# A two-block transformer kernel on one core: each engine's order of work taken from a drawn sketch instead of one common list

## The chip, the cores and the metric

The kernel runs on one core of a Trainium2 chip. Five engines work side by side, each through its own fixed instruction stream: TensorE (PE, matrix products), VectorE (DVE), ScalarE (ACT), GpSimd (POOL) and SyncE (SP, which issues the DMA transfers). They meet only at semaphores. The metric is the device time of one launch in microseconds.

## The reference

The input `x` is 1024 wide with 512 tokens, a context adds 256 tokens. `first_block` is one layer:

```python
x = x + 0.5 * rms_norm(swiglu(rms_norm(x, ffn1_pre_g), ffn1_w_gu, ffn1_w_down), ffn1_post_g)
y = hybrid_mixer(rms_norm(x, mix_pre_g), ...)    # RG-LRU recurrence beside windowed attention
x = x + rms_norm(y, mix_post_g)
x = x + 0.5 * rms_norm(swiglu(rms_norm(x, ffn2_pre_g), ...), ffn2_post_g)
```

The second block has two layers on latents and context. Each is a mixer and a feed-forward network with a `layer_norm` (mean, variance, root) behind each sum, shifts, scales and gates from a conditioning vector (`modulate`), and a mixer that is retention in the first layer and neighbourhood attention in the second. All products are fp32.

## The kernel before

**Tiling.** Activations lie transposed: 128 partitions hold one of 8 chunks of the width (`c`), the free axis holds tokens. A product of 1024 inputs to 128 outputs is an `mm` item: 8 steps `k`, each of three matmuls (`products`, L1463 to L1465), since every fp32 operand is held as a high and a low part and the products low·high, high·low, high·high are added in one PSUM bank. Tokens come as one group of 512 or two of 256 (`s`).

**Who does what.** SP loads weights into a ring of three raw tiles. ACT casts a raw tile to its high part (`prep`, L1723); DVE (L2018) or POOL (L2477) subtracts to get the low part (`prep_lo`). TensorE multiplies. DVE or ACT drain the PSUM bank: `up` and `gate` make the hidden tile (L2149 product, L2152 its low part, L1787 the activation), `down_f` (L2162) and `gated` (L2173) take the outputs. DVE also works out the modulation, 192 operations `ada` (L2107, 128x1024), spread through the program.

**Norms.** A norm over the width is a chain across three engines. Squares (ACT L1731, L1733) are added up (DVE `sum`, L2038). On TensorE `root_sum` (L1549) adds over the partitions by short matmuls, ACT takes the root (L1738), DVE turns and spreads it (`root_diag`, L2044, L2048), and TensorE's `root_row` (L1557) puts it in a bank. From there DVE scales (`norm_apply` L2079, `norm_add` L2086, or `ln_apply` L2092), and the sends (ACT L1744, L1768, L1770; DVE L2066, L2098) write the next matmul's operand `t_h`, high and low. A layer norm has a `mean` (TensorE L1538, L1540) ahead.

**What sets the order.** `schedule()` emits one Python list `items`. The norm chains are generators that yield hand-written delays in microseconds; `tick(us)` is called as the matmul work is emitted and steps each chain whose delay is over, `force` steps a chain to its end where its result is needed. `root`, which places `root_sum`, `root_diag` and `root_row`, reads:

```python
    put("root_sum", inst=inst, s=s, eps=eps, bank=b, before=before, col=i % 4 * 2)
    yield 2.4
    ...
    put("root_diag", inst=inst, s=s, off=off, after=after, col=i % 4 * 2)
    ...
    yield 1.2
    put("root_row", inst=inst, s=s, off=off, bank=b)
```

All five programs then walk that one list with `for it in items: if it.kind in part: part[it.kind](it)`. So an item's place in the list is its place on every engine that has a part in it; an engine never passes an item whose semaphore isn't there yet. The stretches of the program, in order: f1 (to about 386 us), the hybrid mixer, f2, retention, f3, neighbourhood attention, f4.

Of the kernel before, what the change touches and what calls it, by code (L numbers as in the profile page):

```python
# [63 lines left out]
ONCE = (0, 2048, 8704)  # L64
VSTART = {0: 0, 128: 1, 256: 2, 384: 3, 64: 4, 192: 5, 320: 6}
# [33 lines left out]
class Lane:  # L99


    def __init__(self, engine, board):
        self.engine, self.board, self.passed = engine, board, {}

    def wait_ge(self, name, key):
        if not self.board.real:
            return
        s = self.board[name]
        v = s.when[key]
        if self.passed.get(name, 0) < v:  # L110
            self.passed[name] = v
            self.engine.wait_ge(s.sem, v)

# [18 lines left out]
def schedule():  # L132
# [4 lines left out]
    lows, adds = [], []  # L137
    where, low, closing, closed, coming = {}, {}, set(), {}, itertools.count()
# [227 lines left out]
    def sum_add(inst, s, c, tile, ready, square, after=(), late=False):  # L366
        it = dict(inst=inst, s=s, c=c, tile=tile, ready=ready, square=square, after=list(after), off=0, keys=[])
        if square:
# [129 lines left out]
    def ffn(f, gu, dn, parts, segs, subs, ends, ver, down, scaled, between=None, first=6, whole=1, steps=together, begun=None, per=32, ahead=None):  # L498
# [13 lines left out]
        for pi, size in enumerate(parts):  # L512
# [13 lines left out]
            def up_post(k, pi=pi, over_hid=over_hid):  # L526
                def post(g):
# [3 lines left out]
                        turned=f == "f3" and pi == len(parts) - 1 and g.n == 512,  # L531
                        los=[(f, pi, k, s) for s in range(g.t0 // 256, (g.t0 + g.n) // 256)])
# [64 lines left out]
    def first_mixer():  # L597
# [27 lines left out]
        def scores(n):  # L625
# [3 lines left out]
            put("att_scores", n=n, before=before, after=[w_free[2 * n], w_free[2 * n + 1]])  # L629
# [201 lines left out]
    def retention():  # L831
# [18 lines left out]
        def queries_keys(h):  # L850
            first = {}

            def post(g, w, k):
# [4 lines left out]
                else:  # L858
# [6 lines left out]
                    put("qk_rope", w=w, h=h, g0=first["g"], b0=first["bank"], g=g.id, bank=g.bank, offs=offs, slots=before, after=ov["qk"])  # L865

# [35 lines left out]
        def finish(h, t0, n):  # L902
# [4 lines left out]
            put("ret_finish", h=h, t0=t0, n=n, bank=b, before=seat(b, "drain_act", ("ret_rs", h, t0)), offs=[v[0] for v in t[t0]], after=rs_after)  # L907

# [469 lines left out]
def sync_program(e, w, S, m, dram, items, loads):  # L1378
# [22 lines left out]
    for it in items:  # L1401
# [59 lines left out]
def tensor_program(e, w, S, m, items):  # L1461
# [239 lines left out]
    for it in items:  # L1701
# [4 lines left out]
def scalar_program(e, w, S, m, items):  # L1706
# [289 lines left out]
    for it in items:  # L1996
# [4 lines left out]
def vector_program(e, w, S, m, items):  # L2001
# [136 lines left out]
    def up(it):  # L2138
# [8 lines left out]
        if it.turned:  # L2147
            out, s, ps = t.rearrange("p (c r) -> p c r", r=8), s.rearrange("p (r c) -> p c r", c=64), ps.rearrange("p (r c) -> p c r", c=64)
        e.tensor_tensor(out, s, ps, ALU.mult).then_inc(  # L2149
            *S["drain_dve"].of(it.g, ("up", it.f, *it.los[0][1:3], it.t0)))  # L2150
        w.wait_ge("hid_hi", it.los[0])
# [120 lines left out]
    def att_scores(it):  # L2272
        nk = P if it.n == 0 else 2 * P
        w.wait_ge("d_misc", "mask1")
        for kv in range(2):
# [67 lines left out]
    def qk_rope(it):  # L2343
# [3 lines left out]
        for half in range(2):  # L2347
# [9 lines left out]
            e.tensor_tensor(u, u, v, ALU.subtract if half == 0 else ALU.add).then_inc(*S["qk"].of((h, wq, half)))  # L2357
        wait_all(it.after)
# [36 lines left out]
    def ret_finish(it):  # L2395
        h, t0, n, rs = it.h, it.t0, it.n, m.rs(it.t0, it.n)
# [3 lines left out]
        e.tensor_tensor(a, a, m.tmp(it.offs[2], n), ALU.add).then_inc(*S["ret_dve"].of(("s", h, t0)))  # L2400
        w.wait_ge("drain_act", ("ret_rs", h, t0))
# [17 lines left out]
    def na_scores(it):  # L2419
        for hd in range(2):  # L2420
            k, key = it.at[hd], (it.half, it.p, hd)
            w.wait_ge("na_ps", ("s", *key))
            w.wait_ge("bm", (it.half, it.c, BKIND[it.b], hd))
# [21 lines left out]
    def na_o(it):  # L2445
# [7 lines left out]
            "mod_send": mod_send, "norm_apply": norm_apply, "norm_add": norm_add, "ln_apply": ln_apply, "ln_send": ln_send, "ada": ada, "ada_add": ada_add, "gate": gate, "up": up,  # L2453
            "down_f": down_f, "gated": gated, "mix_lambda": mix_lambda, "mix_pad": mix_pad, "scaled": scaled, "conv": conv, "rec_l": rec_l, "rec_c": rec_c,
            "rec_e": rec_e, "rec_g": rec_g, "att_scores": att_scores, "att_probs": att_probs, "att_out": att_out, "mix_apply": mix_apply, "mix_lo": mix_lo,
            "ret_setup": ret_setup, "ret_decay": ret_decay, "qk_rope": qk_rope, "qk_ctx": qk_ctx, "rows_split": rows_split,
            "ret_score": ret_score, "ret_low": ret_low, "ret_y": ret_y, "ret_split": ret_split, "ret_copy": ret_copy,
            "ret_finish": ret_finish, "na_scores": na_scores, "na_probs": na_probs, "na_y": na_y, "na_o": na_o}
    w.wait_ge("d_par", 0)
    for it in items:  # L2460
# [4 lines left out]
def gpsimd_program(e, w, S, m, items):  # L2465
# [40 lines left out]
    for it in items:  # L2506
# [19 lines left out]
def build_program(nc, ins, out):  # L2526
    with ExitStack() as ctx:
# [10 lines left out]
        def run(program, e, *a):  # L2538
            program(e, Lane(e, S), S, m, *a)

        programs = ((sync_program, (dram, items, loads)), (tensor_program, (items,)), (scalar_program, (items,)),
                    (vector_program, (items,)), (gpsimd_program, (items,)))
        for program, a in programs:
            run(program, Quiet(), *a)
# [4 lines left out]
        def _(e):  # L2549
            run(programs[0][0], e, *programs[0][1])  # L2550

        @block.tensor
        def _(e):
            run(programs[1][0], e, *programs[1][1])

        @block.scalar
        def _(e):
            run(programs[2][0], e, *programs[2][1])

        @block.vector  # L2560
        def _(e):
            run(programs[3][0], e, *programs[3][1])

        @block.gpsimd
        def _(e):
            run(programs[4][0], e, *programs[4][1])
# [95 lines left out]
```

## Time and profile before

| | |
|---|---|
| runs | 2977.07, 2978.41, 2978.04 us |
| median | 2978.04 us |
| span of the profiled execution | 2969.8 us |
| median less that span | 8.2 us |
| mean granted TensorE clock | 0.986 of full |
| DMA | 268.84 MB, mean 91 GB/s |

No time beside its span is recorded for the profiled execution itself; the 8.2 us between the span (first to last instruction) and the median of the runs is taken as what lies around it.

A row of a timeline reads: start, length, engine, line and operation, output <- inputs with partitions x elements, and in brackets the idle time of the engine just before with what ended it. A matmul's length is that of its own pipeline; two that follow each other start closer together than they are long.

### The profile page before, as it was taken

The numbers are of one execution on the slowest core, as the hardware profiler recorded it, in microseconds if no ns is written. First come the engines' busy times: TensorE is split into PE (matmuls) and PEld (weight loads), VectorE is DVE, ScalarE is ACT, GpSimd is POOL, SyncE is SP. The second block draws the span as 40 slices with busy tenths as digits, with TensorE's granted clock in tenths as the row PEclk, the third lists the DMA queues.
The fourth block names the chain that finished last, engine by engine and source line by source line (L and its number), as shares of the span: only waits on it lengthen the run. The fifth ranks groups of instructions, "written<-read, shape, count | busy, mean of one in ns | idle before, by whom it ended". The sixth has DMA issues, their size and how long they took to land.

```text
span 2969.8 us, 40717 instructions
## 1 busy us (share of the span) xinstructions
PE 2860.4 (96%) x16352; PEld 2484.7 (84%) x16352; DVE 1536.3 (52%) x2689; ACT 1079.2 (36%) x1873; POOL 540.6 (18%) x287
## 2 busy tenths in 40 slices
PE   8999989999999999999999899999999989999998
PEld 7888886988878888888888888888887777988887
DVE  5667468656674643434446543543564525642224
ACT  5322247543323542423324622112245435442222
POOL 2333200023332011110111011111102212122210
PEclk9999999999999999999999999999999999999999
DMA  4554312225443111121111032322422121133331
GB/s 163 170 163 156 113 59 79 79 83 177 148 160 114 66 56 58 37 71 36 57 57 50 30 106 94 116 92 84 142 70 77 47 71 49 65 93 101 99 99 36
DMA packets 84715, 268.84 MB, mean 91 GB/s; under 512 B 9008, under 2 KB 16560, under 8 KB 84144
## 3 DMA queue, kind: packets, MB, share of 16 engines
q1 hardware_dynamic: 84528, 266.25, 27.8%
q8 instruction: 129, 2.11, 0.3%
q14 instruction: 58, 0.48, 0.1%
HBM read 262.54 MB, written 2.10 MB: 89 GB/s over the span
## 4 chain that ended last, share of the span: by engine, by line
PE 61%; DVE 4%; ACT 2%; issue 1%; DMA 0%; DVEq 0%; ACTq 0%
PE ps L1463 19%; PE ps L1464 19%; PE ps L1465 19%; PE ps L1691 1%; PE ps L1675 1%; PE ps L1664 1%; DVE t_m L2038 1%; ACT t_whi L1723 1%; DVE t_m L2061 0%; ACT t_h L1770 0%; DVE t_wlo L2018 0%; PE ps L1557 0%; ACT t_tmp L1970 0%; DVE t_x L2061 0%; DVE t_x L2173 0%
## 5 line engine op out<-in xcount | busy, mean ns | idle before, releaser
L1463 PE MATMUL ps<-t_h,t_whi 128*128 128x512 f32 (+1 forms) x2320 | 810.5, 349 | 12.8 <-DVE t_h L2066 9.5
L1464 PE MATMUL ps<-t_h,t_wlo 128*128 128x512 f32 (+1 forms) x2320 | 805.6, 347 | 0.0
L1465 PE MATMUL ps<-t_h,t_whi 128*128 128x512 f32 (+1 forms) x2320 | 804.6, 347 | 0.0
L2477 POOL TENSOR_TENSOR t_wlo<-t_raw,t_whi 128x1024 fp32r<-128x1024 f32 (+3 forms) x144 | 350.9, 2437 | 1465.4 <-ACT t_whi L1723 1465.2
L1463 PEld LDWEIGHTS ps<-t_h,t_whi 128*128 128x128 f32 x2320 | 442.6, 191 | 74.6 <-issue 16.1
L1464 PEld LDWEIGHTS ps<-t_h,t_wlo 128*128 128x128 f32 x2320 | 442.7, 191 | 54.3 <-issue 1.0
L1465 PEld LDWEIGHTS ps<-t_h,t_whi 128*128 128x128 f32 x2320 | 442.3, 191 | 54.1
L1723 ACT CAST t_whi<-t_raw 128x1024 fp32r<-128x1024 f32 (+3 forms) x322 | 321.0, 998 | 306.9 <-PE ps L1465 258.7
L1463 PE MATMUL ps<-t_hid,t_whi 128*128 128x256 f32 (+1 forms) x1298 | 423.0, 326 | 6.6 <-DVE t_hid L2152 4.3
L1464 PE MATMUL ps<-t_hid,t_wlo 128*128 128x256 f32 (+1 forms) x1298 | 420.3, 324 | 0.0
L1465 PE MATMUL ps<-t_hid,t_whi 128*128 128x256 f32 (+1 forms) x1298 | 419.5, 323 | 0.0
L2018 DVE TENSOR_TENSOR t_wlo<-t_raw,t_whi 128x1024 fp32r<-128x1024 f32 (+3 forms) x178 | 219.3, 1233 | 261.0 <-ACT t_whi L1723 260.6
L2107 DVE CUSTOM_DVE_ANT_0 t_m<-t_raw,t_m 128x1024 f32<-128x1024 f32 x192 | 302.3, 1611 | 49.9 <-DMA t_raw<-in_ada 39.3
L1463 PEld LDWEIGHTS ps<-t_hid,t_whi 128*128 128x128 f32 x1298 | 248.5, 191 | 28.4 <-DVE t_hid L2152 4.5
L1464 PEld LDWEIGHTS ps<-t_hid,t_wlo 128*128 128x128 f32 x1298 | 248.6, 192 | 19.1
L1465 PEld LDWEIGHTS ps<-t_hid,t_whi 128*128 128x128 f32 x1298 | 248.3, 191 | 19.1
L2149 DVE TENSOR_TENSOR t_tmp<-t_m,ps 128x512 f32<-128x512 f32 (+1 forms) x121 | 72.7, 601 | 310.3 <-PE ps L1465 265.4
L1796 ACT CAST t_hid<-t_tmp 128x512 fp32r<-128x512 f32 (+1 forms) x121 | 65.7, 543 | 368.0 <-DVE t_tmp L2149 368.0
L2152 DVE TENSOR_TENSOR t_hid<-t_tmp,t_hid 128x512 fp32r<-128x512 f32 (+1 forms) x121 | 92.4, 764 | 73.9 <-ACT t_hid L1796 73.9
L2483 POOL TENSOR_TENSOR t_m<-t_m,t_tmp 128x512 f32<-128x512 f32 (+1 forms) x49 | 62.7, 1280 | 328.4 <-ACT t_m L1787 328.4
L1463 PE MATMUL ps<-t_wlo,t_h 128*128 128x512 f32 x264 | 103.9, 394 | 0.4 <-DVE t_m L2425 0.4
L1463 PE MATMUL ps<-t_h 128*128 128x512 f32 (+1 forms) x256 | 94.0, 367 | 10.5 <-DVE t_m L2162 10.5
(290 smaller groups left out, 4142.2 us busy)
## 6 DMA issues: line engine op xcount, KB each, us to landing
t_raw<-in_gu SPq DMA_DIRECT2D x176, 512.0 KB, 3.3
t_raw<-in_ada SPq DMA_DIRECT2D x96, 512.0 KB, 3.4
t_raw<-in_dn SPq DMA_DIRECT2D x52, 512.0 KB, 3.7
t_raw<-in_dn SPq DMA_DIRECT2D x24, 384.0 KB, 3.3
t_raw<-in_ret_v SPq DMA_DIRECT2D x16, 512.0 KB, 4.3
t_raw<-in_ret_qk SPq DMA_DIRECT2D x16, 512.0 KB, 3.4
t_raw<-in_ret_g SPq DMA_DIRECT2D x16, 512.0 KB, 3.3
t_raw<-in_ret_o SPq DMA_DIRECT2D x16, 512.0 KB, 3.8
```

The lines of the kernel that those rows point to most:

```text
L1463: e.matmul(out, whi, xlo, start=first, stop=False, skip_group_check=shared)
L1464: e.matmul(out, wlo, xhi, start=False, stop=False, skip_group_check=shared)
L1465: return e.matmul(out, whi, xhi, start=False, stop=last, skip_group_check=shared)
L1664: done = e.matmul(m.PS[:, hd, o:o + 256], m.na_q(it.c, it.b * P, P)[pp], m.na_k(it.c, keys, 256)[pp], start=True, stop=True, skip_group_ch ...
L1723: e.copy(m.block(0, it.slot, math.prod(it.shape)), m.raw(it)).then_inc(*S["hi"].of(j))
L1796: e.copy(m.hid(0, it.k, it.pitch, it.t0, it.n), m.tmp(it.off, it.n)).then_inc(*S["hid_hi"].of(it.los[0]))
L2018: e.tensor_tensor(m.block(1, it.slot, n), m.raw(it), m.block(0, it.slot, n), ALU.subtract).then_inc(*S["lo_dve"].of(j))
L2107: e.tensor_tensor_reduce(m.at(ADA_OUT + who * 1024, 1024), m.RAW[:, it.raw % NR, :], m.cond(who), 1.0, 0.0, ALU.mult, ALU.add, m.mod(it.la ...
L2149: e.tensor_tensor(out, s, ps, ALU.mult).then_inc(*S["drain_dve"].of(it.g, ("up", it.f, *it.los[0][1:3], it.t0)))
L2152: e.tensor_tensor(m.hid(1, it.k, it.pitch, it.t0, it.n), t, m.hid(0, it.k, it.pitch, it.t0, it.n), ALU.subtract).then_inc(*S["hid_lo"].of( ...
L2477: e.tensor_tensor(m.block(1, it.slot, n), m.raw(it), m.block(0, it.slot, n), ALU.subtract).then_inc(*S["lo_pool"].of(j))
L2483: e.tensor_tensor(s, s, m.rs(it.t0, it.n), ALU.mult).then_inc(*S["gate_pool"].of(it.key, *((it.f, "rs", h) for h in halves(it.t0, it.n))))
```

## The change

A new class `Plan` first draws the five programs without emitting anything: every engine call is recorded as an `Op` with the events it waits for and a length from a formula in its shape. Then `arrange` works back from TensorE's order to give each operation a time at which it is due, and `run` plays the five engines forward. Each time an engine is free it takes, among the items that could begin, the one due soonest. Operations of one `(kind, inst, s)` keep their order among themselves; SP's and TensorE's main order stay. `mean`, `root_sum` and `root_row` float on TensorE: they are taken as soon as what they wait for is there, also between two steps `k` of an `mm` item (`between`). The real programs then follow these orders. Some items are split so that their halves can be placed apart (`up` and `up_lo`, `qk_rope` and `qk_lo`, `ret_finish` and `ret_recip`), some waits that the common order had implied are written out (`acc_read`, `ready_x`, `misc_free`, `nsink`, `bm`), and `mm` waits for its low weights behind the wait for its operand.

```diff
+    FLOATING = ("mean", "root_sum", "root_row")
...
+        n = math.prod(out.shape[1:])
+        if self.engine == "tensor":
+            if name == "transpose" or n == 1:
+                takes = 109
+            elif a[1].dtype == F32R:
+                takes = max(n / 2.4 + 13.3, 109)
+            else:
+                takes = 2 * max(2 * n / 2.4 + 2.5, 109)
...
+            lasts = takes + 165
+        elif self.engine == "scalar":
+            takes = 110 + 0.8 * n
+            lasts = takes + 95
...
+        elif self.engine == "vector":
+            takes = 6.55 * n if name == "reciprocal" and n > 64 else 1150 if n == 1024 else 65 + 1.05 * n
+            if name == "scalar_tensor_tensor":
+                takes += 60
+            lasts = takes + 85
+        elif self.engine == "gpsimd":
+            takes = 150 + 2.2 * n
+            lasts = takes + 60
+        else:
+            takes, lasts = 480, 3300
...
+                        some = [q for q in heads[engine] if q and q[0][0].at <= t and self.opens(q[0])]
+                        if engine in ("scalar", "vector", "gpsimd"):
+                            some = [q for q in some if q[0][0].due < t + 60000]
...
+                        if engine == "tensor":
+                            q = min(some, key=lambda q: self.family(q[0][0]) == ("main",))
+                        else:
+                            q = min(some, key=lambda q: q[0][0].due)
...
+                    if op.table is not None and op.table != table:
+                        table, takes, lasts = op.table, takes + 1283, lasts + 1283
...
     def mm(it):
         out = m.PS[:, it.bank, 0:it.n]
-        w.wait_ge(it.lo, it.w)
         for k in range(it.nk):
+            if k:
+                for x in w.between(it, k):
+                    part[x.kind](x)
             xhi, xlo = moving(it, k)
             if k == 0:
+                w.wait_ge(it.lo, it.w)
                 wait_all(it.before)
...
-    for it in items:
+    for it in w.turns(items):
         if it.kind in part:
             part[it.kind](it)
```

The numbers of instructions stay as they were on PE, DVE, POOL and SP; ACT has 56 `ACT_TABLE_LOAD` where it had 49. Lines of the changed kernel are 270 to 285 higher: the products are L1733 to L1735, `root_row` L1830, `prep_lo` L2291, `sum` L2311, `down_f` L2438.

**VectorE at the end of f1.** The rows are DVE's, `L2162` (now `L2438`) being the drains of the last output columns, whose banks the mixer's first products wait for, and `L2018` (now `L2291`) low parts of the mixer's weights. Before:

```order
L2066 SCALAR_TENSOR_TENSOR t_h<-t_x,t_par,t_h 128x256 [waits h_hi]
L2086 TENSOR_TENSOR t_x<-t_x,t_m 128x256 [waits f_scaled]
L2066 SCALAR_TENSOR_TENSOR t_h<-t_x,t_par,t_h 128x256 [waits h_hi]
L2162 TENSOR_TENSOR t_m<-t_m,ps 128x256 [waits ps]
L2038 TENSOR_TENSOR t_m<-t_m,t_tmp 128x256 [waits sq,acc]
L2018 TENSOR_TENSOR t_wlo<-t_raw,t_whi 128x1024 [waits hi,d_ring2]
L2066 SCALAR_TENSOR_TENSOR t_h<-t_x,t_par,t_h 128x256 [waits h_hi] x2
L2162 TENSOR_TENSOR t_m<-t_m,ps 128x256 [waits ps]
L2038 TENSOR_TENSOR t_m<-t_m,t_tmp 128x256 [waits sq,acc]
L2018 TENSOR_TENSOR t_wlo<-t_raw,t_whi 128x1024 [waits hi,d_ring0]
L2162 TENSOR_TENSOR t_m<-t_m,ps 128x256 [waits ps]
L2038 TENSOR_TENSOR t_m<-t_m,t_tmp 128x256 [waits sq,acc] x2
```

and with the change:

```order
L2339 SCALAR_TENSOR_TENSOR t_h<-t_x,t_par,t_h 128x256 [waits h_hi]
L2352 SCALAR_TENSOR_TENSOR t_m<-t_m,t_par,ps 128x256 [waits drain_dve]
L2438 TENSOR_TENSOR t_m<-t_m,ps 128x256 [waits ps]
L2339 SCALAR_TENSOR_TENSOR t_h<-t_x,t_par,t_h 128x256 [waits h_hi]
L2359 TENSOR_TENSOR t_x<-t_x,t_m 128x256 [waits f_scaled]
L2291 TENSOR_TENSOR t_wlo<-t_raw,t_whi 128x1024 [waits hi,d_ring2]
L2339 SCALAR_TENSOR_TENSOR t_h<-t_x,t_par,t_h 128x256 [waits h_hi]
L2438 TENSOR_TENSOR t_m<-t_m,ps 128x256 [waits ps]
L2291 TENSOR_TENSOR t_wlo<-t_raw,t_whi 128x1024 [waits hi,d_ring0]
L2311 TENSOR_TENSOR t_m<-t_m,t_tmp 128x256 [waits sq]
L2311 TENSOR_TENSOR t_m<-t_m,t_tmp 128x256 [waits sq,acc_act]
L2311 TENSOR_TENSOR t_m<-t_m,t_tmp 128x256 [waits sq,acc] x4
```

Before, each of the last two drains stands behind its own low part of weights, and a sum behind every drain; now one low part is left between the drains of the excerpt, and the sums come together behind the last drain.

**TensorE at the start of f3.** `root_row` of the first layer norm's variance (`l00v`, first 256 tokens) stood between the last product of retention's output (`t_hid`) and the first of f3 (`t_h`). Before:

```order
L1463 MATMUL ps<-t_hid,t_whi 128x256
L1464 MATMUL ps<-t_hid,t_wlo 128x256
L1465 MATMUL ps<-t_hid,t_whi 128x256
L1557 MATMUL ps<-t_tmp,t_con 128x128 [waits root_dve]
L1557 MATMUL ps<-t_tmp,t_con 128x128
L1463 MATMUL ps<-t_h,t_mw 128x256 [waits drain_dve,lo_pool,h_lo]
L1464 MATMUL ps<-t_h,t_mw 128x256
```

and with the change, where the main products are the same and the first of f3 follows the last of retention at once:

```order
L1733 MATMUL ps<-t_h,t_whi 128x256
L1734 MATMUL ps<-t_h,t_wlo 128x256
L1735 MATMUL ps<-t_h,t_whi 128x256
L1830 MATMUL ps<-t_tmp,t_con 128x128 [waits root_dve]
L1830 MATMUL ps<-t_tmp,t_con 128x128
L1733 MATMUL ps<-t_h,t_mw 128x256 [waits h_lo]
L1734 MATMUL ps<-t_h,t_mw 128x256
```

It stands 48 matmuls of 256 columns later in the main order.

**VectorE in the neighbourhood attention.** `L2425` (now `L2709`) adds the bias to a block's scores, `L2435` (now `L2719`) scales the probabilities, `L2018` (now `L2291`) is the low part of weights. Before:

```order
L2425 ISA t_m 128x1
L2425 ISA t_m<-ps,t_m 128x512 [waits bm,na_ps]
L2425 ISA t_m 128x1
L2425 ISA t_tmp,t_m<-ps,t_m 128x512 [waits h_lo,hid_lo,bm,na_ps]
L2425 ISA t_m 128x1
L2425 ISA t_tmp,t_m<-ps,t_m 128x512 [waits bm,na_ps]
L2425 ISA t_m 128x1
L2433 RECIPROCAL t_m<-t_m 128x1 [waits na_act]
L2435 TENSOR_SCALAR t_m<-t_m 128x512 [waits na_dve]
L2433 RECIPROCAL t_m<-t_m 128x1 [waits na_act]
L2435 TENSOR_SCALAR t_m<-t_m 128x512 [waits na_dve]
L2018 TENSOR_TENSOR t_wlo<-t_raw,t_whi 128x1024 [waits hi,d_ring1]
```

and with the change:

```order
L2709 ISA t_m<-ps,t_m 128x512 [waits bm,na_ps]
L2709 ISA t_m 128x1
L2709 ISA t_m<-ps,t_m 128x512 [waits bm,na_ps]
L2709 ISA t_m 128x1
L2717 RECIPROCAL t_m<-t_m 128x1 [waits na_act]
L2719 TENSOR_SCALAR t_m<-t_m 128x512 [waits na_dve]
L2717 RECIPROCAL t_m<-t_m 128x1 [waits na_act]
L2719 TENSOR_SCALAR t_m<-t_m 128x512 [waits na_dve]
L2709 ISA t_tmp,t_m<-ps,t_m 128x512 [waits h_lo,hid_lo,bm,na_ps]
L2709 ISA t_m 128x1
L2709 ISA t_tmp,t_m<-ps,t_m 128x512 [waits bm,na_ps]
L2709 ISA t_m 128x1
```

The first block's probabilities now come ahead of the second block's scores, and the low part that stood behind them follows nine rows later.

## Rows read from the trace of the kernel before

**Rows 1.** Page, part 1: busy time, share of the span and instructions of each engine.

```profile
PE 2860.4 (96%) x16352; PEld 2484.7 (84%) x16352; DVE 1536.3 (52%) x2689; ACT 1079.2 (36%) x1873; POOL 540.6 (18%) x287
```

**Rows 2.** Waits of PE: waiting line <- releaser: us in total, times, longest.

```profile
PE ps L1557 <- DVE t_tmp L2048: 25.0, 11, 7.8
PE ps L1549 <- DVE t_m L2038: 14.5, 6, 4.8
PE ps L1664 <- DVE t_m L2425: 11.5, 6, 4.3
PE ps L1463 <- DVE t_m L2162: 10.5, 1, 10.5
PE ps L1463 <- DVE t_h L2066: 10.0, 2, 9.5
PE ps L1664 <- ACT t_m L1807: 4.8, 1, 4.8
PE ps L1463 <- DVE t_hid L2152: 4.3, 1, 4.3
PE ps L1598 <- ACT t_m L1867: 4.0, 3, 3.2
PE ps L1463 <- DVE t_h L2098: 2.7, 1, 2.7
```

**Rows 3.** Thirteen windows, two and the sum: PE, PEld, DVE, ACT, POOL busy, clock, DMA.

```profile
1644.10:1654.30 10.20, 4.81 (x22) 4.81 (x23) 9.28 (x20) 7.69 (x17) 0.00 (x0) 0.50 0.32 105
...
2958.20:2969.80 11.60, 3.09 (x12) 2.71 (x12) 4.22 (x13) 3.56 (x9) 0.00 (x0) 0.50 0.27 90
sum 82.60, PE 55.45 PEld 51.15 DVE 54.17 ACT 44.49 POOL 6.21; mean PE 4.27 PEld 3.93 DVE 4.17 ACT 3.42 POOL 0.48
```

**Rows 4.** Timeline of PE, 383 to 398 us: start, length, instruction.

```profile
385.77 0.28 PE L1464 MATMUL ps<-t_hid,t_h 128*128 128x256 f32 x1
385.89 0.28 PE L1465 MATMUL ps<-t_hid,t_h 128*128 128x256 f32 x1
...
397.04 0.42 PE L1464 MATMUL ps<-t_h 128*128 128x256 f32 x1
397.25 0.41 PE L1465 MATMUL ps<-t_h 128*128 128x256 f32 x1
```

**Rows 5.** Timeline of DVE and ACT, 390 to 397 us.

```profile
394.98 1.23 DVE L2018 TENSOR_TENSOR t_wlo<-t_raw,t_whi 128x1024 fp32r<-128x1024 f32 x1 [1.15 <-ACT t_whi L1723]
396.12 0.41 DVE L2162 TENSOR_TENSOR t_m<-t_m,ps 128x256 f32<-128x256 f32 x1
...
393.53 0.42 ACT L1733 ACTIVATE t_tmp<-t_m 128x256 f32<-128x256 f32 x1 [1.68 <-DVE t_m L2162]
393.85 1.03 ACT L1723 CAST t_whi<-t_raw 128x1024 fp32r<-128x1024 f32 x1
```

**Rows 6.** Timeline of ACT and DVE, 1644 to 1650 us.

```profile
1644.88 0.24 ACT L1738 ACTIVATE t_st<-ps,t_con 128x2 f32<-128x2 f32 x1
...
1648.76 0.16 DVE L2044 RECIPROCAL t_st<-t_st 128x2 f32<-128x2 f32 x1
```

**Rows 7.** Timeline of PE, end of the program.

```profile
2958.61 1.87 PE L1549 MATMUL ps<-t_con,t_m 128*128 128x1 f32 x8 [4.84 <-DVE t_m L2038]
```

**Rows 8.** Timeline of ACT, 24 to 26 us.

```profile
24.01 1.28 ACT L1787 ACT_TABLE_LOAD   x1
```

**Rows 9.** Groups by form: busy, mean ns of one, idle before and releaser.

```profile
L2107 DVE CUSTOM_DVE_ANT_0 t_m<-t_raw,t_m 128x1024 f32<-128x1024 f32 x192 | 302.3, 1611 | 49.9 <-DMA t_raw<-in_ada 39.3 <-ACT t_m L1714 10.3
L1970 ACT ACTIVATE t_tmp<-t_tmp,t_m 128x512 f32<-128x512 f32 x40 | 28.6, 715 | 22.0 <-DVE t_m L2425 22.0
L2038 DVE TENSOR_TENSOR t_m<-t_m,t_tmp 128x256 f32<-128x256 f32 x132 | 50.3, 432 | 10.5 <-ACT t_tmp L1733 10.5
```

**Rows 10.** Timeline of POOL and DVE, 1610 to 1613 us.

```profile
1610.29 2.40 POOL L2477 TENSOR_TENSOR t_mw<-t_raw,t_mw 128x1024 fp32r<-128x1024 f32 x1 [2.29 <-ACT t_mw L1723]
...
1610.40 2.57 DVE L2038 TENSOR_TENSOR t_m<-t_x 128x256 f32<-128x256 f32 x1
```

More of the change, by code:

```diff
@@ L4 @@
 import numpy as np
+from collections import deque
 from contextlib import ExitStack
@@ L99, with __init__, turns, between @@
 class Lane:
-    def __init__(self, engine, board):
+    def __init__(self, engine, board, order):
         self.engine, self.board, self.passed = engine, board, {}
+        self.order, self.inside = [], {}
+        inner = []
+        for it, piece in order:
+            if piece:
+                self.inside[it.id, piece] = inner
+                for x in inner:
+                    self.order.remove(x)
+                inner = []
+            elif it.kind in Plan.FLOATING:
+                self.order.append(it)
+                inner.append(it)
+            else:
+                self.order.append(it)
+                inner = []
+    def turns(self, items):
+        return self.order
+    def between(self, it, k):
+        return self.inside[it.id, k]
     def wait_ge(self, name, key):
@@ L112, in wait_ge, with insort, __init__, of @@
             self.engine.wait_ge(s.sem, v)
+def insort(some, x):
+    lo, hi = 0, len(some)
+    while lo < hi:
+        mid = (lo + hi) // 2
+        if some[mid] < x:
+            lo = mid + 1
+        else:
+            hi = mid
+    some.insert(lo, x)
+class Mark:
+    def __init__(self, name, plan):
+        self.name, self.plan = name, plan
+    def of(self, *keys):
+        for k in keys:
+            self.plan.made[self.name, k] = self.plan.ops[self.plan.engine][-1]
+        return self, 0
@@ new lines, with __init__, __getattr__, take @@
+class Op:
+    def __init__(self, engine, item, piece, waits, takes, lasts, table):
+        self.engine, self.item, self.piece, self.waits = engine, item, piece, waits
+        self.takes, self.lasts, self.table = takes, lasts, table
+        self.then, self.due, self.at, self.done = [], LATE, 0.0, False
+class Sketch:
+    def __init__(self, plan):
+        self.plan = plan
+    def __getattr__(self, name):
+        def take(*a, **k):
+            if name != "then_inc":
+                self.plan.note(name, k["out"] if "out" in k else a[0], a)
+            return self
+        return take
@@ L367, in sum_add @@
         it = dict(inst=inst, s=s, c=c, tile=tile, ready=ready, square=square, after=list(after), off=0, keys=[])
+        if c < 2 if square else 2 <= c < 4:
+            it["after"] += acc_read.get(s, [])
         if square:
@@ L1700, in tensor_program @@
     w.wait_ge("d_par", 0)
-    for it in items:
+    for it in w.turns(items):
         if it.kind in part:
@@ L1995, in scalar_program @@
     w.wait_ge("d_par", 0)
-    for it in items:
+    for it in w.turns(items):
         if it.kind in part:
@@ L2505, in gpsimd_program @@
     w.wait_ge("d_par", 0)
-    for it in items:
+    for it in w.turns(items):
         if it.kind in part:
@@ L2536, in build_program, with run @@
         items, loads = schedule()
[L2538 to L2544, printed above, removed]
+        programs = (("sync", sync_program, (m, dram, items, loads)), ("tensor", tensor_program, (m, items)),
+                    ("scalar", scalar_program, (m, items)), ("vector", vector_program, (m, items)),
+                    ("gpsimd", gpsimd_program, (m, items)))
+        plan = Plan()
+        plan.draw(programs)
+        order = plan.arrange()
+        def run(k, e):
+            name, program, a = programs[k]
+            program(e, Lane(e, S, order[name]), S, *a)
+        for k in range(5):
+            run(k, Quiet())
         S.again()
```

179 lines of the change are left out of this document (167 added, 12 removed).

## The prediction

> **What bounds the kernel now.** I read the page's busy times first: TensorE is busy 96% of the span, VectorE 52%, ScalarE 36% [rows 1]. So the order of work on the other engines can win only what TensorE loses to waits and to its clock; the 2860.4 us of its own busy time stay, but for the part run slowly.
>
> Second, the waits of TensorE [rows 2]. Nine rows give 87.3 us; thirteen smaller ones, 2.5 the largest, make it 102.3. I sort them by what the change can reach.
>
> - **Floats**: `root_row` 25.0, `root_sum` 14.5, `mean` 0.9 (a small row): 40.4 us. These matmuls stand at a place in TensorE's queue that a delay in microseconds chose, and all main products wait behind them. Some 6.6 lie in the tail, where nothing is left to put ahead (4.84 in one piece [rows 7]). 33.8 are left.
> - **Order stalls** of main products, 52.4: the neighbourhood attention 18.7 (11.5 and 4.8 [rows 2] and 2.4 in small rows), the end of f1 10.5, the mixer some 8 (4.0 on L1598 [rows 2], 3.9 in small rows), retention 5.5 in small rows, the end of f2 4.3, f4's start 2.7, POOL's low parts 2.5.
> - **The start**, 9.5 of the 10.0 on L2066, waits for the first input. It stays.
>
> Third, the clock. Thirteen windows have a granted clock of 0.50, the lower of the two levels (1.2 of 2.4 GHz); the other stretches are at full. In them TensorE is busy 55.45 us, 3.09 of it in the tail [rows 3]. All but one of the windows begin in a wait of TensorE or right behind one. Products of 256 columns start 0.12 us apart at the end of f1 and 0.21 apart behind the 10.5 us wait [rows 4]. So 52.4 us of work outside the tail cost about twice what they should: 26 us are lost to the clock beside the waits.
>
> Fourth, two places show why the waits are there. At the end of f1 the order is a ladder: ScalarE's square waits for VectorE's drain, the next weights' cast stands behind the square, VectorE's low part waits 1.15 us for that cast, and the next drain stands behind the low part, until the last at 396.12 frees TensorE [rows 5]. These rows are the last rung; each is some 3 to 4 us, and none needs the one before. At the start of f3 ScalarE has the root at 1645.12 (1644.88 plus 0.24), yet VectorE takes the reciprocal at 1648.76 [rows 6], since other items stand ahead of it; `root_row` waits 7.8 us, and f3's products behind it.
>
> **The change, part by part.**
>
> *Floats.* `root_row` of f3's first variance goes behind 48 matmuls of 256 columns, 48 x 0.12 = 5.8 us of work at full clock [rows 4] (11.5 us at the 0.24 of half), and VectorE's side is reordered too, so the 7.8 go. Other floats move by up to 72 matmuls either way, most to where their operand is expected. Bounds: nothing if the products that overtake need the float's own result, all 33.8 if it always has cover. I take 28; the 4.80 near the program's start has little to put ahead. Effect: -28.
>
> *Order stalls.* The end of f1: the sums no longer stand among the drains and one low part leaves them, -10.5. In the mixer half, -4; f2's end has its last hidden tile as the true end of a chain, -2; POOL's low parts -2.5; retention and f4's start 0 (chains of the algorithm); the neighbourhood attention a third, -6, since the first block's probabilities now precede the second block's scores, which helps the next products but puts a wait for ScalarE at VectorE's head. Together -25; bounds 0 and -52.
>
> *Waits that come.* ScalarE's first weight cast now stands behind four sends and a square, which may start TensorE about 1 us later. Seven more table loads at 1.28 [rows 8] are 9.0 us on an engine that is 64% idle; between 0 and 9.0 on the path. Float matmuls placed too early are new waits. I take +1 for the start and +5 for the rest.
>
> The Trainium skill, "ScalarE: Activation LUTs", section "What ACT_TABLE_LOAD costs", says that a switch costs a drain besides the load, 2.66 us in all; seven would be 18.6. By that the upper end of this term, and the sum at worst, would be 9.6 us higher.
>
> *Everything else moved* (weights' casts and low parts, ada, drains in the FFNs) costs nothing where TensorE works through columns without waits: f2, f3 and f4 have hardly a row in the waits, since casts and low parts run columns ahead of it. If that cover went, each low part of 1.2 us would show.
>
> *Clock.* 53 of the 86 us of waits outside start and tail go; the clock's 26 go in proportion, 16. Bounds 0 and 26.
>
> Sum: -28 - 25 + 1 + 5 - 16 = -63. The profiled span of 2969.8 becomes 2906.8; with the 8.2 us between span and median, 2978.0 - 63 = **2915 us**.
>
> Best case: 34 of floats, 40 of stalls, 24 of the clock and nothing new, 98 less: 2880.
>
> **Rivals.**
>
> *A: the sketch's lengths are too short.* An item taken as ready is not, and on a real engine all behind it waits. An exp over 128x512 with its accumulated sum is 110+0.8x512 = 520 ns in the sketch; the trace has 715 for the exp alone [rows 9]. VectorE now stands at the reciprocal behind two such exps before it may touch the next block's scores. A VectorE sum that runs beside a POOL low part took 2.57 us [rows 10] against a mean of 0.43 [rows 9]; the sketch has no such term. With 32 block pairs at 2 x 0.2 us, the attention loses 12 us instead of winning 6. Floats then give 20, f1's end 10.5, other stalls 0, the clock 6: -20 - 10.5 + 12 - 6 = -24.5, 2954. For it: these rows. Against: in the FFNs slack of whole columns absorbs it.
>
> The Trainium skill, "GPSIMD Engine Reference", section 8, says that GpSimd shares its SBUF interfaces with VectorE and that VectorE instructions with two SBUF inputs contend with it. By that rule moves onto other neighbours change lengths everywhere, as here; the trace agrees at 1610 us.
>
> *B: VectorE's backlog is the limit where the long floats are.* In the window from 1644.1 it is busy 9.28 of 10.2 us [rows 3]. If the operand `t_h` of f3's products is simply late, the wait moves from `root_row` to them. The two places of that kind have 7.8 and 7.0 us and smaller ones of 2.2; those 17 and 5 of the clock stay: -63 + 22 = -41, 2937.
>
> *C: slower, by `ada`.* Its 192 operations take 1611 ns [rows 9] and 1150 in the sketch. Where one stands right ahead of a drain that TensorE waits for, it makes that 0.46 us late. 192 x 0.46 = 88 us if every one does: 2978 - 63 + 88 = 3003. The place is block 2's FFNs and mixers; it decides from 137 of the 192 (63 / 0.46), and below some 30 it is not seen. Against: TensorE has six banks in turn, so one late drain is not waited for, and before no wait is put down to an `ada`.
>
> *D: the change does not do what it says.* The orders come out so alike that only places off the path move: 2978. Against: the order of all five stalls above is seen to differ.
>
> **How the numbers follow.** Forecast 0.60, A 0.16, B 0.12, C 0.07, D 0.05. A measurement of this kernel tells about 0.2%, 6 us, from no change. Faster by more: forecast, B and A, 0.88; same: D, 0.05; slower: C, 0.07. The range takes the best case as its lower end, 2880. Above it must leave out no more than 0.2: C, D and half of A are that, so it ends a little above A's time, at 2960. The forecast's own range is 2880 to 2945.
>
> **What would show it.** Right: TensorE's waits fall from 102.3 to about 55; the row of `root_row` on its releaser falls from 25 to under 5; the 10.5 us wait at the end of f1 is gone; the windows of half clock fall to five or so; busy time of VectorE and ScalarE as before, plus 9 us of table loads. A shows as TensorE waits on the scores (L2709) of the attention growing, with VectorE idle on ScalarE's exp; B as waits of L1733 for `t_h` near 1650 and 2220 us; C as many small waits on drains with `ada` just before them. Wrong altogether, if TensorE's waits stay above 90 us or new rows over 5 us appear in the FFNs.

## The result and the profile after

The changed kernel takes **2897.89 us** (median of 4 runs, 2897.53 to 2898.70) against 2978.09 us for the kernel before (4 runs), a ratio of 0.9736 with a 95% interval of 0.9724 to 0.9748. It is 80 us faster; 63 were forecast, with a range that holds the time.

The page of the changed kernel, part 1, to be read beside [rows 1]:

```profile
PE 2842.3 (98%) x16352; PEld 2469.1 (85%) x16352; DVE 1549.7 (53%) x2689; ACT 1093.3 (38%) x1880; POOL 542.6 (19%) x287
```

TensorE's busy time is 18.1 us less with the same instructions, which is the clock. VectorE's is 13.4 us more and ScalarE's 14.1, 9.0 of that the seven table loads. TensorE's waits (line <- releaser: us in total, times, longest), to be read beside [rows 2]:

```profile
PE ps L1733 <- DVE t_wlo L2291: 11.6, 1, 11.6
PE ps L1733 <- DVE t_hid L2428: 9.3, 4, 8.0
PE ps L1822 <- DVE t_m L2311: 6.2, 4, 4.8
PE ps L1830 <- DVE t_tmp L2321: 4.8, 5, 1.2
PE ps L1937 <- DVE t_m L2709: 2.5, 6, 0.7
...
PE ps L1813 <- DVE t_m L2311: 1.9, 3, 1.0
PE ps L1811 <- DVE t_m L2311: 1.8, 1, 1.8
...
PE ps L1937 <- ACT t_m L2080: 0.8, 1, 0.8
...
PE ps L1733 <- DVE t_m L2438: 0.7, 1, 0.7
```

TensorE's idle time is 47.6 us in all, from 102.3; the rows of this view hold 46.8 of it, the rest are gaps too short for a row. The floats (L1822, L1830, L1813, L1811) have 14.7 left of 40.4, and the largest piece of that is the tail's 4.8, as before [rows 7]. The 10.5 at the end of f1 is 0.7 (L2438). The attention's scores (L1937) fell from 11.5 and 4.8 to 2.5 and 0.8. Two rows are larger: the start, 11.6 from 9.5, and a new one of 8.0 in f1, for `up_lo` (L2428), the low part of a hidden tile.

The windows at the half clock (busy of PE, PEld, DVE, ACT, POOL, then the granted clock), to be read beside [rows 3]:

```profile
340.20:350.30 10.10, 3.88 (x10) 2.78 (x11) 7.57 (x12) 2.32 (x4) 2.11 (x1) 0.50 0.44 156
517.60:524.40 6.80, 6.80 (x33) 6.80 (x33) 3.08 (x10) 2.12 (x5) 0.00 (x0) 0.50 0.00 0
1579.00:1582.50 3.50, 3.50 (x19) 3.50 (x18) 3.13 (x9) 2.08 (x6) 0.00 (x0) 0.52 0.00 0
2883.00:2896.90 13.90, 3.09 (x12) 2.71 (x12) 6.56 (x20) 4.78 (x13) 0.00 (x0) 0.50 0.23 75
sum 34.30, PE 17.27 PEld 15.79 DVE 20.34 ACT 11.30 POOL 2.11; mean PE 4.32 PEld 3.95 DVE 5.08 ACT 2.82 POOL 0.53
```

Four windows are left of thirteen. Outside the tail, 14.2 us of products run at 1.2 GHz in place of 52.4, so some 7 us are lost and not 26. One of them comes with the new wait and one (1579.0) behind a wait of 1.8 us; one (517.6) comes in a stretch where TensorE is busy throughout and had waited only 0.7 us in one piece, some 2 us before, and why it is there stays open.

**Where the new wait comes from.** VectorE (start, length, instruction, idle before and releaser):

```profile
336.73 0.17 DVE L2467 TENSOR_SCALAR t_m<-t_m 128x4 f32<-128x4 f32 x1 [14.05 <-ACT t_m L2092]
...
340.74 0.17 DVE L2488 TENSOR_SCALAR t_m<-t_m 128x4 f32<-128x4 f32 x1
340.82 0.69 DVE L2409 TENSOR_TENSOR t_m<-ps,t_tmp 128x512 f32<-128x512 f32 x1
341.43 0.68 DVE L2422 TENSOR_TENSOR t_tmp<-t_m,ps 128x512 f32<-128x512 f32 x1
342.02 3.42 DVE L2291 TENSOR_TENSOR t_wlo<-t_raw,t_whi 128x1024 fp32r<-128x1024 f32 x2
345.36 0.68 DVE L2428 TENSOR_TENSOR t_hid<-t_tmp,t_hid 128x512 fp32r<-128x512 f32 x1
```

and ScalarE in the same stretch:

```profile
334.13 1.05 ACT L1996 CAST t_whi<-t_raw 128x1024 fp32r<-128x1024 f32 x1 [4.39 <-PE ps L1735]
335.19 1.28 ACT L2092 ACT_TABLE_LOAD   x1
336.49 0.21 ACT L2092 ACTIVATE t_m<-t_m 128x4 f32<-128x4 f32 x1
```

The item `mix_lambda`, the decay of the mixer's recurrence, has one exp on ScalarE and 21 dependent operations of 0.2 us after it on VectorE, all one block that nothing may interrupt. It isn't needed until the mixer. VectorE reached it early and stood 14.05 us at its head for an exp that ScalarE's order has behind two casts, each of which waits 4.39 us for TensorE. Then the block, the last gate and two low parts stood ahead of `up_lo`, and TensorE, out of work at 338.1, went on at 346.1.

### The profile page after: what moved, and what is told of

Its sections match the earlier page's. It is cut to its first block, busy times and chain, and to the rows that moved or that the text cites. A ratio compares the mean times of both kernels' runs of the same rounds, so it can differ in the third digit from the quotient of the medians.

```text
span 2896.9 us, 40773 instructions
## 1 busy us (share of the span) xinstructions
PE 2842.3 (98%) x16352; PEld 2469.1 (85%) x16352; DVE 1549.7 (53%) x2689; ACT 1093.3 (38%) x1880; POOL 542.6 (19%) x287
## 4 chain that ended last, share of the span: by engine, by line
PE 90%; DVE 4%; ACT 4%; issue 1%; DMA 0%; POOL 0%; DVEq 0%; ACTq 0%; SPq 0%; POOLq 0%
PE ps L1733 29%; PE ps L1734 28%; PE ps L1735 28%; PE ps L1937 1%; PE ps L1964 1%; PE ps L1948 1%; ACT t_whi L1996 1%; DVE t_m L2311 1%; DVE t_wlo L2291 1%; PE ps L1822 1%; ACT t_h L2043 0%; PE ps L1830 0%; ACT t_tmp L2041 0%; DVE t_x L2449 0%; DVE t_m L2334 0%
## 5 line engine op out<-in xcount | busy, mean ns | idle before, releaser
L1733 PE MATMUL ps<-t_h,t_whi 128*128 128x512 f32 (+1 forms) x2320 | 807.4, 348 | 12.4 <-DVE t_wlo L2291 11.6
L1735 PE MATMUL ps<-t_h,t_whi 128*128 128x512 f32 (+1 forms) x2320 | 802.5, 346 | 0.0
L2761 POOL TENSOR_TENSOR t_wlo<-t_raw,t_whi 128x1024 fp32r<-128x1024 f32 (+3 forms) x144 | 342.2, 2377 | 1501.6 <-ACT t_whi L1996 1501.6
L1733 PEld LDWEIGHTS ps<-t_h,t_whi 128*128 128x128 f32 x2320 | 440.3, 190 | 71.9 <-issue 18.2
L1735 PEld LDWEIGHTS ps<-t_h,t_whi 128*128 128x128 f32 x2320 | 440.1, 190 | 54.2
L1733 PE MATMUL ps<-t_hid,t_whi 128*128 128x256 f32 (+1 forms) x1298 | 422.1, 325 | 0.6 <-DVE t_hid L2428 0.6
L1735 PE MATMUL ps<-t_hid,t_whi 128*128 128x256 f32 (+1 forms) x1298 | 419.5, 323 | 0.0
L2291 DVE TENSOR_TENSOR t_wlo<-t_raw,t_whi 128x1024 fp32r<-128x1024 f32 (+3 forms) x178 | 216.6, 1217 | 129.3 <-ACT t_whi L1996 129.0
L1733 PEld LDWEIGHTS ps<-t_hid,t_whi 128*128 128x128 f32 x1298 | 248.2, 191 | 21.5 <-issue 0.9
L1735 PEld LDWEIGHTS ps<-t_hid,t_whi 128*128 128x128 f32 x1298 | 248.1, 191 | 19.2
L2428 DVE TENSOR_TENSOR t_hid<-t_tmp,t_hid 128x512 fp32r<-128x512 f32 (+1 forms) x121 | 114.8, 953 | 33.7 <-ACT t_hid L2069 33.3
L1733 PE MATMUL ps<-t_wlo,t_h 128*128 128x512 f32 x264 | 103.6, 393 | 0.0
L1734 PE MATMUL ps<-t_whi,t_h 128*128 128x512 f32 x264 | 102.9, 390 | 0.0
L1735 PE MATMUL ps<-t_whi,t_h 128*128 128x512 f32 x264 | 102.8, 389 | 0.0
```

Of the source, the lines that this page charges most:

```text
L1733: e.matmul(out, whi, xlo, start=first, stop=False, skip_group_check=shared)
L1734: e.matmul(out, wlo, xhi, start=False, stop=False, skip_group_check=shared)
L1735: return e.matmul(out, whi, xhi, start=False, stop=last, skip_group_check=shared)
L2291: e.tensor_tensor(m.block(1, it.slot, n), m.raw(it), m.block(0, it.slot, n), ALU.subtract).then_inc(*S["lo_dve"].of(j))
L2428: e.tensor_tensor(m.hid(1, it.k, it.pitch, it.t0, it.n), t, m.hid(0, it.k, it.pitch, it.t0, it.n), ALU.subtract).then_inc(*S["hid_lo"].of( ...
L2761: e.tensor_tensor(m.block(1, it.slot, n), m.raw(it), m.block(0, it.slot, n), ALU.subtract).then_inc(*S["lo_pool"].of(j))
```

## The experiments

Each run is compared with runs of the kernel before on the same chip in the same session; those medians were 2975.0, 2976.4, 2977.2 and 2976.4 us. The runs of e1, e4 and e8 spread over 5 to 9 us, those of e2, e3, e7 and e10 over 3 to 5.4, those of the others over 1.3 at most.

**e1, all orders from the list.** In `family`, and floats off:

```diff
+        if op.engine in ('scalar', 'vector', 'gpsimd'):
+            return ("main",)
...
-    FLOATING = ("mean", "root_sum", "root_row")
+    FLOATING = ()
```

> The changed kernel with every engine in the order of the one list and no float; the split items, the written-out waits and the later wait for low weights stay. Theory 1 (the new orders make the whole gain): as before, 2978 within 2 us, TensorE's waits some 102 us with the 10.5 and 7.8 us ones back. Rival (a part of the gain comes from the split items or the moved wait for low weights): 2 to 10 us faster than before.

Measured: 2976.1 us, ratio 1.0005 (0.9995 to 1.0014). The waits of 10.5, 7.9 and 6.9 us are back:

```profile
PE ps L1832 <- DVE t_tmp L2323: 23.5, 11, 7.9
...
PE ps L1735 <- DVE t_m L2440: 10.5, 1, 10.5
```

The split items, the written-out waits and the later wait for low weights cost and give nothing that this interval, some 3 us to either side, can show; the gain is order, that of the other engines' queues and that of the floats.

**e2, the floats alone.** The same lines in `family`, `FLOATING` kept.

> ScalarE, VectorE and GpSimd in the list's order; mean, root_sum and root_row float on TensorE. Theory 1 (floats and order add up, 28 us of waits and some 9 of clock by the floats): about 2941. Rival (the floats' operands come late because VectorE's order holds them, so moving the matmul alone only takes the products out from behind it and soon they want the norm themselves): 2955 to 2970, with waits of the products for t_h in place of root_row's.

Measured: 2951.2 us, ratio 0.9930 (0.9913 to 0.9946), between the two expectations. The floats' own waits fell, but the products took some of them over. Waits of TensorE in e2:

```profile
PE ps L1735 <- DVE t_h L2341: 11.8, 2, 9.1
PE ps L1735 <- DVE t_m L2440: 11.6, 1, 11.6
...
PE ps L1824 <- DVE t_m L2313: 7.7, 3, 4.8
PE ps L1735 <- DVE t_hid L2430: 7.6, 2, 4.3
...
PE ps L1735 <- DVE t_wlo L2293: 3.6, 2, 2.9
PE ps L1832 <- DVE t_tmp L2323: 3.0, 3, 1.1
```

`root_row` (L1832) has 3.0 of 25.0 us, `root_sum` (L1824) 7.7 of 14.5; `mean` grew from 0.9 to 3.9, so the floats together went from 40.4 to 14.6. New are 2.7 for `t_h` (11.8 with the start's 9.1), 3.3 for `t_hid` and 2.1 for `t_wlo` beyond what stood in their rows: products that had been held back by a float now reach the next late operand sooner.

**e3, the orders alone.** Only `FLOATING = ()`.

> ScalarE, VectorE and GpSimd in the sketch's order, made with mean, root_sum and root_row at the list's places on TensorE. Theory 1: the order stalls' 31 us and their clock go, floats' waits stay near 30: about 2937. Rival (the sketch's order on VectorE brings root_diag early enough that even fixed floats hardly wait): 2910 to 2920, floats' waits under 15 us.

Measured: 2912.1 us, ratio 0.9795 (0.9781 to 0.9810): the rival's side, though the floats' waits are 17.8 us, a little above its 15. Waits of TensorE in e3:

```profile
PE ps L1822 <- DVE t_m L2311: 13.3, 4, 4.8
PE ps L1733 <- DVE t_wlo L2291: 11.0, 1, 11.0
PE ps L1733 <- DVE t_hid L2428: 11.0, 3, 9.9
...
PE ps L1830 <- DVE t_tmp L2321: 3.8, 3, 1.6
```

`root_row` at its old place waits 3.8 us in place of 25.0, since VectorE takes the reciprocal when the root is there. At the start of f3 it is this row, 0.30 us behind the root, where before it was 3.6 us late [rows 6]:

```profile
1624.23 0.17 DVE L2317 RECIPROCAL t_st<-t_st 128x2 f32<-128x2 f32 x1 [0.30 <-ACT t_st L2011]
```

The new wait of the changed kernel is here too, as 9.9 us (L2428). So the two remedies overlap. Floats alone give 24 us, orders alone 63, both 80: with the other engines in order the floats have only 14 us (2912.1 to 2897.9) left to win.

**e4, ScalarE's order alone.** `family` returns `("main",)` for VectorE and GpSimd, no floats.

> Only ScalarE in the sketch's order; VectorE and GpSimd in the list's, no floats. Theory 1 (VectorE's queue is what delays TensorE, ScalarE is 36% busy): little, 2965 to 2980. Rival (the ladder at the end of f1 is broken on ScalarE, by the cast that no longer stands behind the square): the 10.5 us wait shrinks to under 4, some 2960.

Measured: 2959.4 us, ratio 0.9957 (0.9942 to 0.9973); the rival was right. From TensorE's waits in e4:

```profile
PE ps L1832 <- DVE t_tmp L2323: 27.6, 9, 9.3
...
PE ps L1735 <- DVE t_m L2440: 3.9, 1, 3.9
...
PE ps L1939 <- ACT t_m L2082: 0.8, 1, 0.8
```

Beside e1, the wait at the end of f1 fell from 10.5 to 3.9, and one of 4.7 in the attention, a copy of ScalarE (`rows_copy`) that stood behind other work, to 0.8. An engine that is 36% busy delayed TensorE by the order of its queue. Against that, `root_row`'s waits grew from 23.5 to 27.6 us and the start's from 9.7 to 11.3. The orders of VectorE and GpSimd beside ScalarE's list were not run. What they do is read from e4 and e3, which both have ScalarE in the sketch's order and no floats: with them `root_row`'s waits go from 27.6 to 3.8 us. VectorE's share and GpSimd's are not told apart.

**e5, the exp earlier.** After `arrange`:

```diff
+        acts = order["scalar"]
+        at = [n for n, (it, _) in enumerate(acts) if it.kind == "mix_lambda"][0]
+        x = acts.pop(at)
+        preps = [n for n in range(at) if acts[n][0].kind == "prep"]
+        acts.insert(preps[-2], x)
```

> The changed kernel, only ScalarE's exp of the recurrence's decay (mix_lambda, L2092) two weight casts earlier. Theory (the new 8.0 us wait at 346 us is VectorE standing 14 us at its head for that exp, and then doing 21 small operations and two low parts ahead of the last gate of f1): VectorE waits in its own idle time, the 8.0 us wait and the half clock behind it (3.9 us window, about 2 us lost) go: 2888. Rival (the wait is for the block's two low parts, which any order puts there, or for the weights' transfer): above 2894.

Measured: 2890.7 us (2890.4 to 2891.1), 7.2 less than the changed kernel (e6, whose time is that of the changed kernel, has 2898.4 in the same session). VectorE's head and TensorE's row for `t_hid` in e5:

```profile
325.42 0.17 DVE L2467 TENSOR_SCALAR t_m<-t_m 128x4 f32<-128x4 f32 x1 [3.17 <-ACT t_m L2092]
```

```profile
PE ps L1733 <- DVE t_hid L2428: 3.0, 4, 1.0
```

The 14.05 us at the head are 3.17, and the 8.0 us wait is 1.0 at most. The cause is shown: one exp of 0.21 us at a place in ScalarE's queue too late for the place that VectorE's queue gives the block. Moving VectorE's block to a later place instead was not run.

**e6, the start on ScalarE.** The setup activation and the first cast are moved to the front of ScalarE's order.

> The changed kernel, ScalarE's setup activation with its table load and the first weight cast put first again. Theory (the start's wait grew from 9.5 to 11.6 since the table load now waits for x and a cast stands behind four sends): TensorE starts 2 us earlier, 2896. Rival (the start is bound by x's transfer, which varies): no change, 2898.

Measured: 2898.4 us, no change. ScalarE was 2 us earlier, but TensorE's first wait is still 11.4, for VectorE's low part: VectorE's order has four sends ahead of it.

```profile
8.46 1.67 DVE L2339 SCALAR_TENSOR_TENSOR t_h<-t_x,t_par,t_h 128x256 fp32r<-128x256 f32 x4 [5.24 <-ACT t_h L2017]
10.05 1.22 DVE L2291 TENSOR_TENSOR t_wlo<-t_raw,t_whi 128x1024 fp32r<-128x1024 f32 x1
```

Neither theory: it isn't the transfer, and not ScalarE alone. e10 puts both engines back.

**e7, lengths from the trace.** In `note`:

```diff
+            takes += 85 * sum(hasattr(k.get(x), "dtype") for x in ("scale", "bias"))
+            if "accum_out" in k:
+                takes += 200
...
+            if name == "tensor_tensor_reduce":
+                takes += 360 if n == 1024 else 85
```

> The sketch's lengths as the trace has them: ada 1510 ns start to start in place of 1150, 85 ns for each per-partition scale or bias on ScalarE, 200 for an accumulated sum. Theory 1 (the orders are insensitive to such errors, since work is columns ahead): within 4 us of 2898. Theory A (wrong lengths put items at the head before they are ready): 6 to 15 us faster.

These lengths are nearer, not true everywhere: an exp over 128x512 with its accumulated sum is 805 ns in them, where the trace of the kernel before has it and its read 0.72 us from start to start; and the 1510 ns of `ada` are a mean over undisturbed and disturbed ones.

Measured: 2890.5 us (2888.4 to 2893.7), 7.4 less: theory A. The 8.0 us wait stayed; the floats' waits went. Those of e7 that are left:

```profile
PE ps L1827 <- DVE t_m L2316: 4.8, 1, 4.8
...
PE ps L1816 <- DVE t_m L2316: 1.8, 1, 1.8
PE ps L1835 <- DVE t_tmp L2326: 1.1, 1, 1.1
PE ps L1818 <- DVE t_m L2316: 0.9, 2, 0.7
```

8.6 us, 6.6 of them the tail's, from 14.7.

**e8 and e9, lengths too short.** All lengths of the three engines in the sketch times 0.7; e9 has `FLOATING = ()` besides.

```diff
+        if self.engine in ("scalar", "vector", "gpsimd"):
+            takes, lasts = 0.7 * takes, 0.7 * lasts
```

> All lengths of ScalarE, VectorE and GpSimd in the sketch times 0.7, so the sketch is far too fast. Theory 1 (insensitive): under 2908. Theory A (an item taken as ready is not, and all behind it waits): 2930 or more, with many waits on drains.

> All lengths of ScalarE, VectorE and GpSimd in the sketch times 0.7 as before, but mean, root_sum and root_row at the list's places on TensorE. Theory B2 (what the short lengths break are the floats, which go into TensorE's queue before their operands are there, and all products wait behind them): the floats' waits of 50 us fall to the 17 of the run with fixed floats, 2915 to 2930. Theory A (VectorE's and ScalarE's own orders go wrong too): above 2945.

Measured: e8 2975.3 us, ratio 1.0003 (0.9994 to 1.0013): the whole gain of 80 us is gone. e9 2948.5 us, ratio 0.9908 (0.9893 to 0.9923). TensorE's waits in e8:

```profile
PE ps L1824 <- DVE t_m L2313: 29.8, 12, 6.2
PE ps L1832 <- DVE t_tmp L2323: 11.2, 7, 4.0
...
PE ps L1735 <- DVE t_m L2440: 6.4, 1, 6.4
PE ps L1873 <- ACT t_m L2142: 6.3, 3, 4.5
```

and in e9:

```profile
PE ps L1824 <- DVE t_m L2313: 21.7, 9, 4.8
...
PE ps L1735 <- DVE t_m L2440: 5.6, 1, 5.6
```

The floats' waits are 49.8 us in e8 and 27.8 in e9, where B2 had 17. Theory A of e8 expected many waits on drains; that row has one of 6.4, and the large rows are the floats'. The split is 27 us for the floats (e9 to e8) and 36 for the orders of VectorE, ScalarE and GpSimd (e3 to e9). So B2 was wrong and the theory A of e9 right: both parts need the lengths. The same freedom that wins 14 us with good lengths loses 27 with short ones, since a float in TensorE's queue ahead of its operand stops every product.

**e11, lengths too long.** The lengths of e7, those of the three engines times 1.1.

> The trace's lengths in the sketch, those of ScalarE, VectorE and GpSimd times 1.1. Theory (errors are one-sided: a float that is sketched too late costs nothing as long as products are left to run, one sketched too early costs at once): within 4 us of the 2890.5 with the trace's lengths, or a little faster. Rival (the order needs true lengths, either error costs alike; times 0.7 cost 77 us): 2905 or more.

Measured: 2882.7 us (2882.4 to 2883.5), 7.8 less than e7. An error of 10% to the long side is harmless here. One of 10% to the short side was not run, and e8's is 30%, so that the short side is the worse one, as the theory has it, is not shown. The 8.0 us wait isn't there, since `mix_lambda` fell elsewhere (its exp at 312.4 us, in e7 at 335.2); in its place the mixer has one of 5.6:

```profile
PE ps L1901 <- ACT t_m L2153: 5.6, 1, 5.6
```

How much of the 7.8 is the margin and how much such luck is open. Small changes of the lengths move single blocks, and one such block was worth 5.6 to 8.0 us in these runs.

**e10, a better version.** The lengths of e7, the move of e5, the one of e6 and on VectorE the first low part ahead of the first send:

```diff
+        vecs = order["vector"]
+        send = [n for n, (it, _) in enumerate(vecs) if it.kind == "rms_send"][0]
+        at = [n for n, (it, _) in enumerate(vecs) if it.kind == "prep_lo"][0]
+        vecs.insert(send, vecs.pop(at))
```

> The sketch with the trace's lengths, the decay's exp two casts earlier on ScalarE, and at the start the setup activation, the first cast and on VectorE the first low part put first. Theory (the gains are at different places and add up: 7.4 for the lengths, 7.2 for the exp, 2 for the start, now that both engines' orders are put back): 2881. Rival (the start's order on VectorE changes nothing either, or the lengths' gain was the same microseconds as the exp's): 2884 to 2890.

Measured: 2880.9 us (2879.8 to 2884.9), ratio to the kernel before 0.9684 (0.9669 to 0.9698), 17 less than the change. It is the sum of the three gains (7.4, 7.2 and 2) to within the 5 us that its runs spread over; the start's 2 us alone were not measured. The start's row is 9.3 again:

```profile
PE ps L1738 <- DVE t_h L2344: 9.3, 1, 9.3
```

**e12, floats between items only.** In `run`, while the main item's next step is ready, floats are not taken:

```diff
+                            if any(self.family(q[0][0]) == ("main",) and q[0][0].piece for q in some):
+                                some = [q for q in some if self.family(q[0][0]) == ("main",)]
```

> The changed kernel, floats taken by TensorE only between whole mm items of 24 matmuls (2.9 or 5.4 us), not between their steps, as long as the item's next step can run. Theory (a float's operand comes at any moment, so it waits half an item more; the norm behind it has slack of some items in most places): 2898 to 2903. Rival (the chain from float to the next operand is tight at every norm, 22 root_sum and 26 root_row): 2908 or more.

Measured: 2898.9 us (2898.6 to 2899.9), 1 us more than the changed kernel. Breaking into an `mm` item is worth next to nothing here.

## Why the prediction was right, and where its terms were off

In the profiled executions the span fell by 72.9 us (2969.8 to 2896.9); the forecast's sum was 63. Its 2915 us is 17 too high, 10 of them by its terms and 7 by the span that it started from. Of its signs, TensorE's waits are 46.8 us (about 55), `root_row`'s 4.8 (under 5) and the windows at half clock four (five or so); VectorE's busy time did not stay as before.

- **Floats**, "-28": measured 33.8 to 8.1 (14.7 less the tail's 6.6), -25.7. The size was right, the reason only in part. The prediction rested this on the 48 matmuls put ahead of `root_row`, with VectorE's reordering as a help; e3 shows that the orders of the other engines take 25.0 to 3.8 with no float moved at all, and e4 that ScalarE's order alone does not (27.6). The row of the late reciprocal [rows 6] had it: a wait of TensorE for an item that was held in VectorE's queue belongs to the order stalls.
- **Order stalls**, "-25": this is the mis-sized term. 52.4 fell to 13.3 without the new wait, -39.1. The attention, for which -6 was taken because VectorE would stand for ScalarE's exp, gave 14.3 (18.7 to 4.4: 2.5, 0.8 and 1.1 in small rows), 3.9 of it by the one copy on ScalarE that e4 wins alone. Retention's chains and f4's start, forecast at 0, gave 2.0 (5.5 to 3.5) and 2.2 (2.7 to 0.5), the mixer 5.8 in place of 4.
- **Waits that come**, "+1" and "+5": +2.1 at the start, of which the prediction knew ScalarE's half and e6 and e10 show VectorE's; +8.0 by `mix_lambda`, which it did not foresee. Of the two things that it took the +5 for, table loads on the path are in no row, and floats placed too early are within the 8.1 above, of which e7 takes 6. That 10 us came where 6 were expected is luck. By its own list of signs a new row over 5 us in an FFN, which this one in f1 is, meant "wrong altogether"; the waits fell to less than half all the same, so that sign was drawn too sharp.
- **Clock**, "-16": 26 to 7, -19.
- Sum by these: -25.7 - 39.1 + 2.1 + 8.0 - 19 = -73.7, against 72.9 in the spans.
- **The 8.2 us around the span** was wrong. Every run here is its span plus 1.8 us (those of e2 plus 2.1). The kernel before just varies: its runs in all sessions went from 2969 to 2980 us, and the profiled execution, 2969.8 and 1.8, was one of the short ones. The last 7 us between 73 and 80 are that. Beside one more trace it is the clock that differs, not the waits: e1, with the orders of the kernel before, was profiled in a span of 2975.3 us, and its waits are 100.5 us beside 102.5, but TensorE's busy time is 7.6 us more:

```profile
PE 2868.0 (96%) x16352; PEld 2491.4 (84%) x16352; DVE 1534.4 (52%) x2689; ACT 1079.1 (36%) x1873; POOL 542.2 (18%) x287
```

**The rivals.** A (short lengths) was there, smaller than priced: 7.4 us by e7, and the attention won 14.3 us where A had it lose 12. As a mechanism it was the right one to fear: lengths of 0.7 take the whole gain (e8).

The changed kernel's trace shows contention too. Of the two low parts at 342.02 the first took 1.22 us; the second began while a GpSimd gate ran, from 342.25 to 344.36, and took 2.28:

```profile
343.16 2.28 DVE L2291 TENSOR_TENSOR t_wlo<-t_raw,t_whi 128x1024 fp32r<-128x1024 f32 x1
```

The Trainium skill, "GPSIMD Engine Reference", section 8, has GpSimd contend with VectorE instructions with two SBUF inputs, on SBUF interfaces that the two share; this row agrees. Contention is also where VectorE's longer busy time comes from: its low parts of hidden tiles of 512 tokens took 849 ns each before and take 1182 now,

```profile
L2428 DVE TENSOR_TENSOR t_hid<-t_tmp,t_hid 128x512 fp32r<-128x512 f32 x77 | 91.0, 1182 | 32.3 <-ACT t_hid L2069 32.3
```

25.6 us more in all, against which other groups need less (`ada` 5.5). Of the 121 such operations of both widths, those with no GpSimd instruction beside them took at most 0.70 us, before and now; the others took 1.44 on average before (25 of them) and take 2.16 now (29).

B (backlog) did not happen; the rows for `t_h` near 1650 and 2220 us are missing. C (`ada`) has no sign: the longest wait for a `down_f` drain is 0.7 us. The 0.46 us it was priced at is contention: in the changed kernel's trace the 117 `ada` operations with no GpSimd instruction beside them took 1.21 to 1.23 us and the other 75 took 2.15 on average, and undisturbed ones start 1148 ns apart. D fell with the measured time. The 1.38 us of drain that the Trainium skill, "ScalarE: Activation LUTs", section "What ACT_TABLE_LOAD costs", adds to a table load isn't seen: in the changed kernel the load of `mix_lambda` began at 335.19, when the cast before it (334.13 and 1.05) had just ended, took 1.28, and its exp starts at 336.49.

## What to carry to other kernels

Where one list orders several in-order queues, read a wait of the bounding engine two steps back: here it was often for an item that was ready and stood behind something that nobody needed yet, on an engine 36% or 52% busy. A planner that mends this is as good as its lengths: 30% too short cost the whole gain (e8), nearer lengths won 7.4 us (e7), and 10% too long lost nothing (e11). If they can't be exact, too long by a little is the tried side; that short errors cost more than long ones of the same size is likely, since a float planned too early stops all products behind it, but it is not shown. A long block of small dependent operations must be started where its partner can serve it at once (e5).

## What was not expected of the hardware

- The clock's share: for 54.7 us less of idle time TensorE's busy time fell by 18.1 us besides, since most waits of a few us that went took their half-clock stretch with them. e10, with 34.9 us of idle time of TensorE in all, has a mean granted clock of 0.997; the profile before has 0.986.
- The kernel before varies by 11 us over all its runs (2969.0 to 2980.5), and its granted clock with them (0.982 to 0.987). That fewer waits make the time steadier does not follow: e9, with 74.3 us of waits, spreads over 0.9 us, e7 and e10, with 41.8 and 34.4, over 5. What sets the spread is open.
